# The first norm as a transpose and a narrow product, and the first two weight tiles of a mixing job taken k by k

## What is computed

```python
def rms_norm(x, g):
    y = x32 * lax.rsqrt(jnp.mean(x32 * x32, axis=-1, keepdims=True) + RMS_EPS)
    return (y * g).astype(x.dtype)
...
x_prev = concatenate([shift[:, None], x[:, :-1]], axis=1)      # x is rms_norm(h, norm_mix[0])
mixed = x[None] + (x_prev - x)[None] * mu[:, None, None, :]    # six mixtures, mu (6, D)
rkv = einsum('jbtd,jde->jbte', mixed[:3], w_rkv)               # r, k, v: D = 1024 each
w_log = -softplus(-(w0 + tanh(mixed[3] @ w1) @ w2)) - 0.5      # w1: D x 64
a = sigmoid(a0 + (mixed[4] @ a1) @ a2)                         # a1: D x 64
g = sigmoid(mixed[5] @ g1) @ g2                                # g1: D x 160
```

## Time and profile before

| | |
|---|---|
| median of 3 runs | 3838.64 us (3832.66 to 3840.56) |
| the profiled execution | 3834.27 us, of which the span is 3831.9 |
| PE busy | 3546.5 us, 93% of the span |
| DVE, ACT, POOL busy | 1285.8, 1005.1, 1660.7 us |
| mean granted clock of TensorE | 0.97 |
| the front phase | about 442 of 3831.9 us |

### The profile page before, as it was taken

One profiled execution on the slowest core, in us unless ns is written; L12 is line 12 of the kernel. 1 busy time (PEld: TensorE's weight loads), 2 busy tenths in 40 slices (PEclk: granted clock), 3 DMA queues, 4 the chain that ended last, 5 costly groups with the idle time before them and its releaser, 6 DMA issues. The chain is left out here.

```text
span 3831.9 us, 82927 instructions
## 1 busy us (share of the span) xinstructions
PE 3546.5 (93%) x34886; PEld 3276.7 (86%) x34886; DVE 1285.8 (34%) x2476; ACT 1005.1 (26%) x2042; POOL 1660.7 (43%) x1184
## 2 busy tenths in 40 slices
PE   7999778888887999999999899999979999999998
PEld 6999667777765999999999877777759999999997
DVE  5112457667752321221222422222233311221223
ACT  5212334545431210000000344444441100000003
POOL 5334355545532444344435533433335344344434
PEclk9999789999996999999999999999989999999999
DMA  3422201111104111111111223233230111111111
GB/s 141 138 87 82 68 22 36 42 46 37 36 24 141 45 45 41 41 42 45 38 38 49 87 84 96 84 93 88 88 121 28 50 50 44 38 44 44 38 38 55
DMA packets 294634, 234.85 MB, mean 61 GB/s; under 512 B 32148, under 2 KB 274084, under 8 KB 293463
## 3 DMA queue, kind: packets, MB, share of 16 engines
q1 hardware_dynamic: 290786, 216.55, 18.4%
q10 hardware_dynamic: 3572, 14.33, 0.9%
HBM read 188.28 MB, written 47.80 MB: 62 GB/s over the span
## 5 line engine op out<-in xcount | busy, mean ns | idle before, releaser
L1964 PE MATMUL ps<-xs,work 128*128 128x384 f32 x6048 | 1051.9, 334 | 0.0
L1964 PEld LDWEIGHTS ps<-xs,work 128*128 128x128 f32 x6048 | 1048.6, 188 | 0.0
L1929 POOL TENSOR_SCALAR work<-work 128x1024 fp32r<-128x1024 f32 x130 | 361.4, 2780 | 938.1 <-PE ps L1977 394.4
L1977 PE MATMUL ps<-work,work 128*128 128x384 f32 x2880 | 502.4, 334 | 0.0
L1977 PEld LDWEIGHTS ps<-work,work 128*128 128x128 f32 x2880 | 499.5, 188 | 0.0
L1172 PE MATMUL ps<-arena 64*64 64x64 f32 (+2 forms) x8800 | 431.9, 237 | 55.2 <-DVE arena L1585 15.5
L1172 PEld LDWEIGHTS ps<-arena 64*64 64x64 f32 x8800 | 324.3, 137 | 90.4 <-issue 35.4
L2455 PE MATMUL ps<-xs,work 128*128 128x384 f32 x1656 | 376.1, 358 | 2.6 <-POOL work L2393 2.6
L2082 DVE TENSOR_TENSOR H<-ps,H 128x1152 f32<-128x1152 f32 x160 | 217.3, 1358 | 479.7 <-PE ps L1977 479.7
L574 PE MATMUL ps<-mixed,wsplit_mix 128*128 128x384 f32 x1872 | 336.1, 340 | 18.3 <-DVE mixed L770 17.7
L1930 POOL TENSOR_TENSOR work<-work,work 128x1024 fp32r<-128x1024 f32 x130 | 346.3, 2664 | 10.9
(11 more groups left out here) (259 smaller groups left out, 4442.4 us busy)
## 6 DMA issues: line engine op xcount, KB each, us to landing
work<-in_ffn_w_gu SPq DMA_DIRECT2D x88, 512.0 KB, 3.8
work<-in_ffn_w_down SPq DMA_DIRECT2D x44, 512.0 KB, 3.2
work<-in_cache_v SPq DMA_DIRECT2D x64, 256.0 KB, 3.7
work<-in_cache_k SPq DMA_DIRECT2D x64, 256.0 KB, 2.8
rkv_scratch<-lora ACTq DMA_DIRECT2D x24, 576.0 KB, 2.8
stage_mix<-in_rwkv_w_rkv SPq DMA_DIRECT2D x24, 512.0 KB, 3.9
work<-in_attn_w_qkv SPq DMA_DIRECT2D x24, 512.0 KB, 4.3
h_scratch<-H SPq DMA_DIRECT2D x2, 4608.0 KB, 14.1
```

The costliest lines, as they stand in the source:

```text
L1929: chain.link(pool.tensor_scalar(w[:, 0, :], mem.stage3[:, slot, :], 1.0, None, ALU.mult))
L1964: last = pe.matmul(ps3[:, c, 0:CW], w[:, part, k * P:(k + 1) * P], mem.xs[:, xpart, k, c * CW:(c + 1) * CW], start=(k == 0 and a == 0), st ...
L1977: last = pe.matmul(BANKS[bank][:, c, 0:CW], mem.wsplit3[:, slots[b], part, k * P:(k + 1) * P], mem.hid[:, b, xpart, c * CW:(c + 1) * CW], ...
```

## The change

In the norm the product by `[identity | diagonal]` is replaced by a PE transpose of the block (`plain`) and a product by the diagonal alone (`normal`), with 128 columns each, in banks of their own. They count two semaphores: `turned` for the plain half, `scaled_rows` for the normalised one. PE's order becomes plain 0, plain 1, normal 0, the vector rows, and then normal i and plain i + 1. ACT's copy to `H` waits for `turned` instead of DVE's product. DVE copies blocks 1, 4 and 6 instead of 2 and 5. ACT takes a square root of eps ahead of everything, which loads the table. GpSimd makes two identity matrices less, and no longer waits for the nine squares.

In the mixing, PE takes the first two tiles of a job together: k of the first tile, and from k = 4 (`LAG`) on, behind it, k - 4 of the second. The weights and banks of the second tile are waited for at k = 4 (`begin`). Only the first tile waits for `lo_done`. The other six tiles run as before. ACT evicts the last tile of the job before, or the low-rank result, ahead of the fifth high part instead of after the eighth.

```diff
--- before.py
+++ after.py
@@ -366,14 +366,15 @@
 ...
     ROWS = T // P
-    BY_DVE = (2, 5)
+    LAG = 4
+    BY_DVE = (1, 4, 6)
     with ExitStack() as ctx:
 ...
         rows_in, x_in = sem("rows_in"), [sem(f"x_in{i}") for i in range(ROWS)]
-        pool_chain, ident_ready, eye_ready, eps_ready = sem("first_chain"), sem("ident_ready"), sem("eye_ready"), sem("eps_ready")
+        pool_chain, ident_ready, scaled_rows, eps_ready = sem("first_chain"), sem("ident_ready"), sem("scaled_rows"), sem("eps_ready")
         squared, root, inverse, diag_ready = sem("squared"), sem("root"), sem("inverse"), sem("diag_ready")
 ...
@@ -402,14 +403,18 @@
 ...
         share = mem.mt1[:, 1, 0:D].rearrange("p (k m) -> p k m", k=KB)
-        eyes = mem.mt2[:, 0, 0:512].rearrange("p (u n) -> p u n", u=2)
+        diagonals = mem.mt2[:, 0, 0:256].rearrange("p (u n) -> p u n", u=2)
         pads = mem.xnp[:, :, PROMPT_PAD + TP:TPAD].rearrange("p k (b t) -> p k b t", b=NS)
 ...
-        def products(i):
-            return mem.ps[:, 4 * (i % 2):4 * (i % 2) + 4, :].rearrange("p b n -> p (b n)").rearrange("p (k n) -> p k n", k=KB)
+        def plain_rows(i):
+            return mem.ps[:, 4 * (i % 2):4 * (i % 2) + 2, :].rearrange("p b n -> p (b n)").rearrange("p (k n) -> p k n", k=KB)
+        def normal_rows(i):
+            return mem.ps[:, 4 * (i % 2) + 2:4 * (i % 2) + 4, :].rearrange("p b n -> p (b n)").rearrange("p (k n) -> p k n", k=KB)
 ...
@@ -477,9 +482,6 @@
 ...
                                base=0, pattern=[[-1, P]], channel_multiplier=1).then_inc(ident_ready, 1)
-            for u in range(2):
-                pool.affine_select(out=eyes[:, u, 0:P], in_=mem.ones[:, :], compare_op=ALU.is_equal, fill=0.0,
-                                   base=0, pattern=[[-1, P]], channel_multiplier=1).then_inc(eye_ready, 1)
             chain.link(pool.memset(mem.headones[:, :], 0.0))
 ...
@@ -491,7 +493,6 @@
 ...
             pool.wait_ge(omu_ready, 1)
-            pool.wait_ge(squared, ROWS)
             turn = 0
 ...
@@ -528,26 +529,38 @@
 ...
             pe.wait_ge(ident_ready, 1)
-            pe.wait_ge(eye_ready, 2)
-            for i in range(ROWS):
+            def plain(i):
                 pe.wait_ge(x_in[i], 16)
-                pe.wait_ge(diag_ready, i + 1)
-                if i == 1:
-                    pe.wait_ge(rows_in, 16 * len(sources))
-                    for k in range(KB):
-                        last = pe.transpose(mem.ps[:, 7, k * NROW:(k + 1) * NROW], mem.rows[0:NROW, k * P:(k + 1) * P], mem.ident[0:NROW, 0:NROW])
-                    last.then_inc(rows_turned, 1)
-                    pe.wait_ge(vec_ready, 1)
                 if i >= 2:
-                    pe.wait_ge(xn_out, i - 1)
                     before = sum(1 for b in BY_DVE if b <= i - 2)
 ...
                         pe.wait_ge(h_dve, before)
-                out = products(i)
                 for k in range(KB):
-                    last = pe.matmul(out[:, k, :], mem.xrow[:, i, k * P:(k + 1) * P], eyes[:, i % 2, :], start=True, stop=True)
+                    last = pe.transpose(plain_rows(i)[:, k, :], mem.xrow[:, i, k * P:(k + 1) * P], mem.ident[:, :])
                 last.then_inc(turned, 1)
+            def normal(i):
+                pe.wait_ge(diag_ready, i + 1)
+                if i >= 2:
+                    pe.wait_ge(xn_out, i - 1)
+                for k in range(KB):
+                    last = pe.matmul(normal_rows(i)[:, k, :], mem.xrow[:, i, k * P:(k + 1) * P], diagonals[:, i % 2, :], start=True, stop=True)
+                last.then_inc(scaled_rows, 1)
+            plain(0)
+            plain(1)
+            normal(0)
+            pe.wait_ge(rows_in, 16 * len(sources))
+            for k in range(KB):
+                last = pe.transpose(mem.ps[:, 7, k * NROW:(k + 1) * NROW], mem.rows[0:NROW, k * P:(k + 1) * P], mem.ident[0:NROW, 0:NROW])
+            last.then_inc(rows_turned, 1)
+            pe.wait_ge(vec_ready, 1)
+            for i in range(1, ROWS):
+                normal(i)
+                if i + 1 < ROWS:
+                    plain(i + 1)
 ...
@@ -563,18 +576,32 @@
 ...
-            def tile(n, v, j):
+            def begin(n):
                 pe.wait_ge(s.w_split, n + 3)
                 pe.wait_ge(ps_free, n + 1)
-                for k in range(KB):
-                    pe.wait_ge(lo_done, KB * j + k + 1)
-                    for a, (w, part) in enumerate(PASSES):
-                        for c in range(3):
-                            last = pe.matmul(mem.ps[:, 4 * v + c, 0:CW], mem.wsplit[:, v, w, k * P:(k + 1) * P],
-                                             mixed[part][:, k, c * CW:(c + 1) * CW],
-                                             start=(k == 0 and a == 0), stop=(k == KB - 1 and a == 2))
-                    last.then_inc(mix_used if k < KB - 1 else s.tile_done, 1)
+            def tile(v, k):
+                for a, (w, part) in enumerate(PASSES):
+                    for c in range(3):
+                        last = pe.matmul(mem.ps[:, 4 * v + c, 0:CW], mem.wsplit[:, v, w, k * P:(k + 1) * P],
+                                         mixed[part][:, k, c * CW:(c + 1) * CW],
+                                         start=(k == 0 and a == 0), stop=(k == KB - 1 and a == 2))
+                last.then_inc(mix_used if k < KB - 1 else s.tile_done, 1)
+            def first_two(n, j):
+                for k in range(KB + LAG):
+                    if k == 0:
+                        begin(n)
+                    if k < KB:
+                        pe.wait_ge(lo_done, KB * j + k + 1)
+                        tile(n % 2, k)
+                    if k == LAG:
+                        begin(n + 1)
+                    if k >= LAG:
+                        tile((n + 1) % 2, k - LAG)
 ...
@@ -584,27 +611,30 @@
 ...
                     last.then_inc(shift_turned, 1)
+                first_two(n0, j)
                 if blocks == 8:
-                    with pe.Fori(0, 4) as i:
+                    with pe.Fori(1, 4) as i:
                         for u in range(2):
-                            tile(n0 + 2 * i + u, (n0 + u) % 2, j)
-                else:
-                    for u in range(blocks):
-                        tile(n0 + u, (n0 + u) % 2, j)
+                            begin(n0 + 2 * i + u)
+                            for k in range(KB):
+                                tile((n0 + u) % 2, k)
 ...
+            act.wait_ge(eps_ready, 1)
+            act.activation(mem.rms[:, 0:1], mem.eps, ACT.Sqrt).then_inc(eps_ready, 1)
             at = 0
 ...
             act.dma_start(bias, t["attn_rel_bias"][0]).then_inc(bias_in, 16)
-            act.wait_ge(eps_ready, 1)
+            act.wait_ge(eps_ready, 2)
             def leave_h(i):
-                act.wait_ge(xn_out, i + 1)
-                act.copy(mem.H[:, :, i * P:(i + 1) * P], products(i)[:, :, 0:P]).then_inc(h_act, 1)
+                act.wait_ge(turned, i + 1)
+                act.copy(mem.H[:, :, i * P:(i + 1) * P], plain_rows(i)).then_inc(h_act, 1)
 ...
@@ -625,7 +655,7 @@
 ...
-            def mix(j, mu):
+            def mix(j, mu, leave_before):
 ...
@@ -647,6 +677,8 @@
 ...
                         scale(k + 1)
+                    if k == LAG:
+                        leave_before()
                     hi(k)
 ...
@@ -696,11 +728,7 @@
 ...
             for j, (mu, blocks, what) in enumerate(MIXED):
-                mix(j, mu)
-                if j:
-                    leave(j - 1, MIXED[j - 1][1] - 1, MIXED[j - 1][1])
-                else:
-                    leave_wa()
+                mix(j, mu, (lambda: leave(j - 1, MIXED[j - 1][1] - 1, MIXED[j - 1][1])) if j else leave_wa)
                 leave(j, 0, blocks - 1)
 ...
@@ -712,20 +740,21 @@
 ...
                 if i >= 2:
-                    dve.wait_ge(turned, i - 1)
-                dve.tensor_scalar(eyes[:, i % 2, P:2 * P], mem.ident[:, :], mem.inv[:, i:i + 1], None, ALU.mult).then_inc(diag_ready, 1)
+                    dve.wait_ge(scaled_rows, i - 1)
+                dve.tensor_scalar(diagonals[:, i % 2, :], mem.ident[:, :], mem.inv[:, i:i + 1], None, ALU.mult).then_inc(diag_ready, 1)
             def leave_x(i):
-                dve.wait_ge(turned, i + 1)
+                dve.wait_ge(scaled_rows, i + 1)
                 gain = mem.vec[:, :, VEC["mix0"]:VEC["mix0"] + 1]
                 if i < TP // P:
-                    dve.tensor_tensor(mem.xnp[:, :, PROMPT_PAD + i * P:PROMPT_PAD + (i + 1) * P], products(i)[:, :, P:2 * P],
+                    dve.tensor_tensor(mem.xnp[:, :, PROMPT_PAD + i * P:PROMPT_PAD + (i + 1) * P], normal_rows(i),
                                       gain.to_broadcast((P, KB, P)), ALU.mult).then_inc(xn_out, 1)
                 else:
-                    dve.tensor_tensor(pads[:, :, :, 1:1 + TS], products(i)[:, :, P:2 * P].rearrange("p k (b t) -> p k b t", b=NS),
```

(4 more changed lines are left out.)

## The result

The changed kernel took 3803.07 us (median of 4 runs, 3801.07 to 3808.33), the kernel before 3839.6 in its 4 runs beside them (3832.66 to 3843.08): a ratio of 0.9913, with a 95% interval of 0.9895 to 0.9930. It is faster, by 36.5 us (0.9%) in these medians. The profiled execution is the slowest of its four: 3808.33, span 3806.3, which is 25.6 less than the span before.

A forecast was written before the change was run, and what follows sets the result against it. The prediction took PE, busy for 93% of the span, to bound the kernel. Norm and projection 15.0 plus mixing 7.9 made 22.9, called 23 us, so 3838.64 - 23 = 3815.6, rounded to 3815, range 3805 to 3826.

The forecast's parts named there:

- The reading: Whole kernel: PE busy 93% of the span, so time is saved where PE idles or its work can be cut.
- The work on PE: Norm: a block of 24 narrow PE instructions at 0.108 each takes 2.6 us.
- The bound with 0.138: Norm: at 0.138 an instruction, a block takes 3.3 us; not taken, since 0.138 holds a drain.
- The start: Norm's start: first product at 8.3 to 9.6, vector rows about 12, normal(1) at 13.4 against 18.09.
- The splits beside the norm: Norm: GpSimd's earlier weight splits slow the last three DVE diagonals, 1.5 us each, with PE waiting; last row at 37.1.
- Rival (c): Norm: every diagonal from the fourth waits for a whole split operation; norm gains 10, total 18, 3820 us; chance 0.12.
- rival (a): Norm: TensorE stays at half clock throughout, 4.8 us a block; only mixing gains, 8 us, 3830 us; chance 0.08.
- Rival (b): Projection: half clock lasts through it too, 41 to 46 us instead of 29.9; 9 us slower, 3847; chance 0.03.
- The projection: Low-rank projection: PE starts at 41.3 against 55.59 and takes about 29.2 us instead of 29.9; norm and projection gain 15.0.
- Mixing: Mixing: PE waits no more from k 4; gains 2.4 in r, 1.6 in k, 2.6 in v, 1.3 in g, sum 7.9.
- rival (d): Mixing: new tile order gains nothing, as the second tile's weights or bank come after k 4; gain 15, 3823.5; chance 0.1.
- The time: Whole kernel: a gain of 23 us, median 3815 us, range 3805 to 3826.

The follow-up runs named there:

- e5: Changed kernel without the early square root of eps, so ACT's table load comes late again: 3812.01 us (1 run).
- e6: Changed kernel with the norm's eight plain transposes per block made as fp32 products with the identity: 3798.10 us (1 run).
- e3: The whole changed kernel once more, unchanged code: 3806.81 us, ratio 0.9928 to the kernel before.
- e8: Changed kernel with the last two tiles of jobs r, k and v also k by k, evictions moved to suit: 3792.47 us, ratio 0.9888 to before.
- e7: Changed kernel with ACT's eviction of the former job's last tile put back behind the eighth high part: 3838.71 us (1 run).
- e9: Repeat of e8, the changed kernel with the last two tiles k by k as well: 3785.01 us, ratio 0.9868 to before.
- e11: Repeat of e6, the changed kernel with plain transposes made as products: 3806.21 us, ratio 0.9924 to before.
- e10: The whole changed kernel a third time, unchanged code: 3810.75 us, ratio 0.9936 to the kernel before.
- e1: Kernel before with only the changed norm, mixing as before: 3806.82 us, ratio 0.9930 to the kernel before.

## Why the prediction was right

**The reading held.** The gain is where PE stood idle and where its work was cut, in the two places named, and what is gained in the front stays. The sum was 15.0 + 7.9 = 22.9; the marks give 15.41 + 9.75 = 25.16.

**The work on PE: right.** 2.6 us for 24 instructions at 0.108 were forecast from the 20 late transposes; the steady blocks take 2.66. The bound with 0.138 was the drain, as argued.

**The start: right, 0.6 us early.** Normal(1) at 13.4 was forecast, 12.76 came. The first product at 8.21 is at the early end of 8.3 to 9.6: ACT's table load is fully hidden. The rows landed at 11.6 where I put 12. The hidden load is worth 2.1 to 2.4 us at the first product (10.65 in e5, 8.21 to 8.59 elsewhere), and nothing that shows at the projection's start.

**The splits beside the norm: right mechanism, a term too large.** I charged the last three diagonals 1.5 us each. They took 0.77, 0.50 and 0.71 instead of 0.29, and PE waited for none of them. From 12.76 the last normal row came out after 23.1 us, 0.6 less than the 23.7 forecast, so it lies 1.2 before the 37.1 forecast. Part of that agreement is luck, as two errors cancel: normal(5) ended 13.7 us after the start (at 26.50) where 12.5 were forecast, among others for a wait of 0.70 at 19.12, and the three blocks behind it took 9.4 where 11.2 were. The 23.7 does not follow from its terms either: 12.5, three blocks of 2.6 and a row of 1.2 are 21.5, which leaves 2.2 for diagonals that were charged at 4.5. The Trainium skill (SBUF — State Buffer, Who interferes with whom) says that the shared pair of ports is an exclusive lock. By that rule the diagonal of 26.34, if it needs the pair, would have had to wait for the end of a GpSimd operation that ran from 25.99 to 28.76; it was through at 27.11, so the trace does not agree for this pair of forms, while the 2.29 in e6, the first lo part of the projection and the 3.38 beside 3.21 in mixing are of the size that the rule asks for. It is no accident of one profile: a diagonal that comes in the first 0.8 us of such an operation (L502) is through 1.12 us after the operation's start in e3, e5 and e8 too. Rival (c) falls, as no diagonal made PE wait, not even one of 1.48 in e8.

**The half clock: rival (a) falls.** In this profile the granted clock is 1.00 from block 1 to the end of the norm, with a third of its instructions transposes and gaps of up to 1.36 us among them. A norm at half clock throughout came in no profile, but one stretch of 3.4 us did, in e5, e7, e8 and e9, which moved the norm's end by under 2 us. Only the first 16 transposes ran at half the pace (3.39 us), where the windows show 1.00. But the trace holds no clock record ahead of 7.41, and a window shows 1.00 where there is none. It is not the transposes either: the first 16 product instructions of the kernel before took 6.14 us instead of 3.7, with a first record at 15.85. The Trainium skill (TensorE: Matmul & The Clock Gate, Part 4: PE-mode transpose) says that transposes do not count as busy for the clock. The trace does not agree: PE had run nothing but transposes since 4.42 when the first products came at 8.21, and these ran at full pace (2.05 us for 16). From PE's first instruction to the first record at 1.00 are 3.0 to 5.9 us in the nine profiles with transposes, and 3.9 and 5.6 in e6 and e11 with products. Rival (b) falls with it: the projection's slow start is 5 us long in both kernels.

**The projection: a wrong step of 0.7 us.** I expected 29.2 instead of 29.9, with DVE's lo parts no longer held up by GpSimd. It took 30.0 (30.4 in e3, 30.0 in e10). The windows show PE busy in every one of these microseconds, so faster lo parts have nothing to give. The 0.7 was taken from the wrong engine. The 29.3 of e1, e7 and e8 come from the shorter stretch at half clock and would have made the number right by luck. The 4.2 us between the last normal row and the projection, taken because GpSimd would run beside them, came out at 4.15. The reason given holds too: in e5, without GpSimd beside the lo part, it is 2.84 (37.97 to 40.81). So the splits' real price is here, 0.9 to 1.3 us in the first lo part, and not in the diagonals. The projection started at 40.05 instead of 41.3, and norm and projection gave 15.4 against 15.0.

**Mixing: right mechanism, the clock mis-sized.** Between the projection's end, the three waits for the fourth part (199.21, 307.65 and 416.08 before, 180.96, 287.27 and 393.38 after) and the front's end, the gains are 2.84 in r (forecast 2.4), 2.13 in k (1.6), 2.32 in v (2.6) and 2.46 in g (1.3). The first two starts of before are these rows:

```profile
199.21 2.47 PE L574 MATMUL ps<-mixed,wsplit_mix 128*128 128x384 f32 x9 [3.20 <-DVE mixed L770]
307.65 1.84 PE L574 MATMUL ps<-mixed,wsplit_mix 128*128 128x384 f32 x9 [3.18 <-DVE mixed L770]
```

In r, PE's wait before the fifth part grew from 0.27 to 0.57 only, where I had put the tanh and its table load at 0.7. In k and g I had carried the slow steps of the profile before over into the changed kernel. In g they took 7.7 us for three steps, at half clock for 6.8 us; in the changed kernel half clock lasts 3.4 us in each of the three jobs. It takes some 1.4 us of PE's time, and 1.03 of these lay under the wait that stood before the next x part, so 0.4 are lost. How long it lasts belongs neither to the job nor to the wait: behind the same 3.2 us it was 3.4 us in k, nothing in v and 6.8 in g in the kernel before, nothing in g in e1, and 6.8 in k and v in e11. To carry the slow steps of one profile over to another kernel was the mistake. ACT's moved eviction cost nothing in k, v and g, as forecast, and the bank was never late: rival (d) falls.

**The time.** The median of 3803.07 lies outside the forecast's 3805 to 3826, by 1.9 us at the lower end, and the step behind that is none of the sum: it is the assumption that a median of a few runs stands within some microseconds of the profile's sum. Measured three times, the same pair of kernels differs by 36.5, 25.4 and 23.5 us in medians, and by 25.6, with 25.2 in the front, in the profiled pair.
